# MLA heads of a streaming encoder in another order: probability tiles grouped, weight split behind the gating, sample output transposed last

## The chip, the cores and the metric

The kernel runs on one core of a Trainium2 chip. The metric is the device time of one execution, in microseconds (us). The median of three runs before the change is 2366.46 us (2363.36 to 2369.05).

## What is computed

One step of a two-layer encoder on two inputs: a prompt of 512 new frames and a sample of 64 frames that continues a cache of 512. Layer 1 is forgetting attention with 16 heads, layer 2 is multi-head latent attention (MLA) with 16 heads; both end with an output projection. The change lies in the MLA heads. Cut to what one head computes there:

```python
kv = einsum('bsc,chd->bshd', c, w_ukv)           # latent (512 wide) to keys and values, 128 + 128 a head
kn, v = _rms_norm(kv[..., :128], g_knope), kv[..., 128:]
logits = (qn @ kn.T + qr @ kr.T) * MLA_SCALE      # 128 content columns, 64 rotary ones
p = softmax(where(chunk-causal mask, logits, NEG_INF))
o = (p @ v) * silu(gate)                          # then x + o @ w_out, after all heads
```

The prompt has 512 queries and keys; the sample has 64 queries over 512 + 64 keys.

## The kernel before, in words

`program` runs blocks one after the other: layer 1, its output projection, the latent and the gates (`block_d`), the queries (`block_e`), the MLA heads (`block_f`, about 1709 to 2145 us of the span) and the output projection (`block_g`). All products are made in fp32r with each operand split into a high and a low half: the high half is copied by ScalarE (ACT), the low half is a subtraction on VectorE (DVE), and three products of halves are added up on TensorE (PE).

`block_f` pipelines the heads: one pass works on the attention of head g = h - 1 and, between its steps, on the up-projection of head h, so that PE has matmuls while ACT and DVE turn one step's result into the next one's operand. `MlaHead.ORDER` lists the steps of a pass, and every engine walks the same list, in its own instruction queue. Pass 0 has no attention, pass 16 has no up-projection, and the 15 passes between have both.

Names that begin with T are tiles of the up-projection. T0 to T7 are 12 matmuls of 256 columns each, four key/value tiles from the prompt and four from the cache, two tiles in a bank (banks 0 to 3); T8 is the sample's own 64 rows, in bank 4. ACT squares the keys of a finished bank (`act_keys`), DVE sums the squares (`dve_sums`), GpSimd (POOL) raises them to the power -0.5 (line 2313), DVE scales the keys (`dve_keys`), and ACT and DVE take the values out as halves (`act_values`, `dve_values`). A T tile may write its bank once the values of the head before are out of it, and T0 also waits for the head's weights: `make_hi` on ACT and `make_lo` on DVE split them (line 195, 128x1024), in one buffer that is free after T7.

The other names are jobs of the attention. `qn`, `kp`, `qr` transpose the prompt's queries, keys and rotary queries; `s3` to `s0` are logits of the four query tiles, `sa` and `sb` the sample's logits in two halves; `p3` to `p0` transpose the probabilities by key tile (1, 2, 3 and 4 transposes), `pn` the sample's; `g` transposes the gate; `o` is the prompt's output (12 matmuls of 512 to 256 columns), `on` the sample's (5 of 256), and `ont` transposes the sample's output after DVE has added its parts and gated it. DVE gates `o` while it takes it out of the bank (`o_mla`, line 2198). Behind its part of `p3` DVE also scales the gate by the softmax sums (`dve_scale_gate`).

Jobs share three PSUM banks (5, 6 and 7) by turns: a job's bank is its index in `JOBS` modulo 3, so each job waits until the job three places before it is out of the bank (`wait_operands`), across the passes too. Who lets a bank go: for jobs that are split, DVE after the low half; for `s` jobs ACT after the exponential; for `g` and `ont` ACT; for `o` and `on` DVE.

```python
        own, k = self.job(name)
        count = {own: k - 1}
```

Of the kernel before, what the change touches and what calls it, by code (L numbers as in the profile page):

```python
# [87 lines left out]
def steps(eng, n, body):  # L88

    body(0, n == 1)  # L90
    if n > 2:
        with eng.Fori(1, n - 1) as i:
            body(i, False)
    if n > 1:
        body(n - 1, True)
# [1800 lines left out]
class MlaHead:  # L1896
# [4 lines left out]


    ORDER = ["qn", "kp", "qr", "T0", "T1", "s3", "ka", "T2", "s2", "new", "T3", "s1", "s0", "T8", "sa", "sb", "T4",
             "p3", "T5", "pn", "p2", "p1", "T6", "on", "p0", "g", "T7", "ont", "o"]
    JOBS = [n for n in ORDER if n[0] != "T"]
    SPLITS = ["qn", "kp", "qr", "ka", "new", "p3", "pn", "p2", "p1", "p0"]
    HALF = [slice(0, NT), slice(NT, 2 * NT + 1)]
# [351 lines left out]
def block_f(c, K, S, tail):  # L2259

    nc, d = c.nc, c.dram
    o_all = c.at("o_mla", [HD, HEADS, SEQ + NEW], F32, c.X)
    wplace, xplace = c.packer(S.f_base), c.packer(c.X + 36864)
    H = MlaHead(c, K, S, wplace, xplace)
    assert wplace.cur[0] <= K.base and xplace.cur[0] <= c.Y, (wplace.cur[0], K.base, xplace.cur[0], c.Y)
    G = H.G
    started = lambda g: not isinstance(g, int) or g > 0

    with nc.Block() as block:
        @block.sync  # L2270
        def _(sp):
            def load_q(g):
                if started(g):
                    H.wait_ready(sp, g - 1, "new")
                sp.dma_start(H.q[:], d["queries"][g]).then_inc(H.q_in.sem, 16)

            def load_gate(g):
                if started(g):
                    H.wait_ready(sp, g - 1, "ont")
                cols = bass.ds(g * HD, HD) if not isinstance(g, int) else slice(g * HD, (g + 1) * HD)  # L2280
                for q, t in ((P, slice(0, NT)), (NEW, slice(SM, TT))):
                    sp.dma_start(H.gate[0:q, t, :], d["gates"][0:q, t, cols]).then_inc(H.g_in.sem, 16)

            G.load(sp, 0, 0)
            G.load(sp, 1, 0)


            tail.sp(sp, HEADS // 2 - 2)
            load_q(0)
            tail.sp(sp, HEADS // 2 - 1)  # L2290
            load_gate(0)
            with sp.Fori(1, HEADS - 1) as h:
                G.load(sp, h + 1, 0)
                load_q(h)
                load_gate(h)
            load_q(HEADS - 1)
            load_gate(HEADS - 1)

        @block.gpsimd
        def _(pool):  # L2300
            pool.memset(H.ss[:], 1.0).then_inc(H.zero.sem, 1)
            pool.memset(H.rs[:], 1.0).then_inc(H.zero.sem, 1)
            pool.memset(H.half[:], -0.5).then_inc(H.zero.sem, 1)
            for x in (H.ptn[:], H.v[:, 2 * NT, :, :], H.pt[NT - 1][0][:], H.pt[NT - 1][1][:]):
                pool.memset(x.bitcast(F32), 0.0).then_inc(H.zero.sem, 1)
            pool.wait_ge(H.zero.sem, 7)
            tail.pool(pool)

            def body(h, last):

                for half, t in enumerate(H.HALF):
                    H.var.wait(pool, h, half + 1)
                    pool.tensor_tensor(H.rstd[:, t], H.ss[:, t], H.half[:, t], ALU.pow).then_inc(H.rst.sem, 1)
            steps(pool, HEADS, body)

        @block.scalar
        def _(act_):
            def body(h, last, g):
                for name in H.ORDER:
                    if name[0] != "T":  # L2320
                        if g is not None:
                            H.act_job(act_, g, name, o_all)
                    elif h is not None:
                        if name in ("T1", "T3", "T5", "T7"):
                            H.act_keys(act_, h, int(name[1]) // 2)
                        elif name == "T8":
                            H.act_new_lo(act_, h)
                        elif name == "T4":
                            H.act_new_keys(act_, h)
                    if h is not None:  # L2330
                        if name == "T7" and not last:
                            G.make_hi(act_, h + 1, 0)


                        if name == "o":
                            H.keys.wait(act_, h, 1)
                            if g is not None:
                                H.wait_ready(act_, g, name)
                            for b in (0, 1):
                                H.act_values(act_, h, b)  # L2340

                    if g is not None and name == "qr":
                        H.keys.wait(act_, g, 2)
                        for b in (2, 3, 4):
                            H.act_values(act_, g, b)
            G.make_hi(act_, 0, 0)
            tail.act(act_)
            body(0, False, None)
            act_.wait_ge(H.zero.sem, 7)
            with act_.Fori(1, HEADS - 1) as h:  # L2350
                body(h, False, h - 1)
            body(HEADS - 1, True, HEADS - 2)
            body(None, True, HEADS - 1)

        @block.vector
        def _(dve):
            for bank_free in H.free:
                bank_free.grant(dve)

            def body(h, last, g):  # L2360
                for name in H.ORDER:
                    if name[0] != "T":
                        if g is not None:
                            H.dve_job(dve, g, name, o_all)
                            if name == "p3":
                                H.dve_scale_gate(dve, g)
                    elif name == "T8" and h is not None:
                        H.dve_new(dve, h)
                    if h is not None:
                        if name == "s0":  # L2370
                            H.dve_sums(dve, h, 0)
                        if name == "sb":
                            H.dve_keys(dve, h, 0)
                        if name == "T7":
                            H.dve_sums(dve, h, 1)
                            if not last:
                                G.make_lo(dve, h + 1, 0)
                        if name == "o":
                            for b in (0, 1):
                                H.dve_values(dve, h, b)  # L2380
                    if g is not None and name == "qr":
                        H.dve_keys(dve, g, 1)
                        for b in (2, 3, 4):
                            H.dve_values(dve, g, b)
            G.make_lo(dve, 0, 0)
            tail.dve(dve)
            dve.wait_ge(H.zero.sem, 7)
            body(0, False, None)
            with dve.Fori(1, HEADS - 1) as h:
                body(h, False, h - 1)  # L2390
            body(HEADS - 1, True, HEADS - 2)
            body(None, True, HEADS - 1)

        @block.tensor
        def _(pe):
            def body(h, last, g):
                for name in H.ORDER:
                    if name[0] != "T":
                        if g is not None:
                            H.pe_job(pe, g, name)  # L2400
                    elif h is not None:
                        H.pe_tile(pe, h, int(name[1]))
            body(0, False, None)
            pe.wait_ge(H.zero.sem, 7)
            with pe.Fori(1, HEADS - 1) as h:
                body(h, False, h - 1)
            body(HEADS - 1, True, HEADS - 2)
            body(None, True, HEADS - 1)
    return o_all
# [122 lines left out]
```

## Time and profile before

| | |
|---|---|
| median of 3 runs | 2366.46 us |
| profiled execution: its time | 2365.76 us |
| profiled execution: its span, first to last instruction | 2364.0 us |
| mean granted clock of TensorE | 0.981 |
| PE busy | 2235.4 us (95%) |
| DVE busy | 1142.2 us (48%) |
| ACT busy | 921.4 us (39%) |
| POOL busy | 216.4 us (9%) |

The page gives one execution. The ends of matmuls are modelled, and successive ones overlap in the rows, so that distances are taken from start to start. Idle time of an engine is listed before the instruction that ended it, with the instruction that released it. Times in the rows are microseconds from the start of the span.

### The profile page before, as it was taken

How to read it: one execution, taken by the hardware profiler on the slowest of the kernel's cores; microseconds unless marked ns; L12 is line 12 of the kernel's file. 1: busy time of each engine (PE TensorE's matmuls, PEld its weight loads, DVE VectorE, ACT ScalarE, POOL GpSimd, SP SyncE). 2: the span in 40 equal slices, each digit the busy share in tenths (PEclk: the TensorE clock that was granted, in tenths of full speed). 3: DMA queues.
4: the chain of work that ended last, by engine and by line, in shares of the span. 5: the costliest groups of instructions: out<-in, count | busy, mean ns of one | idle time of the engine just before them, and what ended most of it. 6: DMA issues, size and time to landing. Idle time of an engine off the chain costs nothing. (4 is left out here: it accounts for less than half of the span.)

```text
span 2364.0 us, 33512 instructions
## 1 busy us (share of the span) xinstructions
PE 2235.4 (95%) x11777; PEld 1896.9 (80%) x11777; DVE 1142.2 (48%) x2633; ACT 921.4 (39%) x1968; POOL 216.4 (9%) x234
## 2 busy tenths in 40 slices
PE   7799999999999999998997999997699999997998
PEld 5688888888888888877887878887689899986887
DVE  5444444444445544552223433224567777774222
ACT  5344444444444444442223333224345555543111
POOL 0100000000000000100000000004721111110000
PEclk9899999999999999999998999998999999998999
DMA  4233333333333323324323222323321111113331
GB/s 159 86 97 100 96 97 98 103 103 103 98 103 101 97 95 100 115 73 143 120 83 122 82 88 100 101 82 117 119 96 44 58 46 51 49 37 129 120 129 68
DMA packets 106110, 225.21 MB, mean 95 GB/s; under 512 B 10384, under 2 KB 45456, under 8 KB 105920
## 3 DMA queue, kind: packets, MB, share of 16 engines
q1 hardware_dynamic: 106048, 224.35, 29.2%
q8 instruction: 42, 0.69, 0.1%
q14 instruction: 20, 0.16, 0.0%
HBM read 191.42 MB, written 32.89 MB: 95 GB/s over the span
## 5 line engine op out<-in xcount | busy, mean ns | idle before, releaser
L216 PE MATMUL bank<-b_whi,x_hi 128*128 128x512 f32 x1024 | 413.5, 404 | 9.6 <-DVE b_wlo L199 9.6
L216 PE MATMUL bank<-b_whi,x_lo 128*128 128x512 f32 x1024 | 402.5, 393 | 0.0
L216 PE MATMUL bank<-b_wlo,x_hi 128*128 128x512 f32 x1024 | 402.4, 393 | 0.0
L199 DVE SCALAR_TENSOR_TENSOR b_wlo<-b_raw,g_fox,b_whi 128x512 fp32r<-128x512 f32 x256 | 180.8, 747 | 131.2 <-ACT b_whi L186 129.1
L216 PEld LDWEIGHTS bank<-b_whi,x_hi 128*128 128x128 f32 x1024 | 193.6, 189 | 47.0 <-DVE b_wlo L199 9.6
L216 PEld LDWEIGHTS bank<-b_whi,x_lo 128*128 128x128 f32 x1024 | 193.2, 189 | 42.2
L216 PEld LDWEIGHTS bank<-b_wlo,x_hi 128*128 128x128 f32 x1024 | 193.7, 189 | 33.8
L186 ACT ACTIVATE b_whi<-b_raw,g_fox 128x512 fp32r<-128x512 f32 x256 | 170.4, 714 | 78.6 <-PE bank L216 59.5
L216 PE MATMUL bank<-m_whi,x_hi 128*128 128x512 f32 x320 | 124.9, 390 | 0.8 <-DVE m_wlo L199 0.8
L216 PE MATMUL bank<-m_wlo,x_hi 128*128 128x512 f32 x320 | 124.6, 389 | 0.0
L216 PE MATMUL bank<-m_whi,x_lo 128*128 128x512 f32 x320 | 124.5, 389 | 0.0
L199 DVE SCALAR_TENSOR_TENSOR m_wlo<-m_raw,g_mla,m_whi 128x512 fp32r<-128x512 f32 x80 | 56.6, 748 | 132.9 <-ACT m_whi L186 132.9
L216 PE MATMUL bank<-c_whi,x_hi 128*128 128x512 f32 x256 | 102.3, 400 | 8.9 <-DVE c_wlo L195 8.9
L186 ACT ACTIVATE m_whi<-m_raw,g_mla 128x512 fp32r<-128x512 f32 x80 | 53.4, 715 | 146.0 <-PE bank L216 146.0
L216 PE MATMUL bank<-g_whi,g_ohi 128*128 128x512 f32 x256 | 100.5, 392 | 7.2 <-DVE g_wlo L195 7.2
L195 DVE TENSOR_TENSOR g_wlo<-g_raw,g_whi 128x1024 fp32r<-128x1024 f32 x32 | 39.2, 1224 | 131.9 <-ACT g_whi L182 131.9
L216 PE MATMUL bank<-b_whi,x_smp 128*128 128x512 f32 x256 | 102.6, 401 | 0.0
L216 PE MATMUL bank<-c_wlo,x_hi 128*128 128x512 f32 x256 | 101.6, 397 | 0.0
L216 PE MATMUL bank<-c_whi,x_lo 128*128 128x512 f32 x256 | 101.4, 396 | 0.0
L216 PE MATMUL bank<-g_wlo,g_ohi 128*128 128x512 f32 x256 | 100.2, 392 | 0.0
L216 PE MATMUL bank<-g_whi,g_olo 128*128 128x512 f32 x256 | 100.1, 391 | 0.0
L216 PE MATMUL bank<-b_wlo,x_smp 128*128 128x512 f32 x256 | 100.0, 391 | 0.0
(465 smaller groups left out, 5024.0 us busy)
## 6 DMA issues: line engine op xcount, KB each, us to landing
b_raw<-w_fox SPq DMA_DIRECT2D x128, 512.0 KB, 3.5
m_raw<-w_mla SPq DMA_DIRECT2D x40, 512.0 KB, 3.5
c_raw<-w_out SPq DMA_DIRECT2D x32, 512.0 KB, 3.5
g_raw<-w_out SPq DMA_DIRECT2D x32, 512.0 KB, 3.5
f_raw<-w_ukv SPq DMA_DIRECT2D x16, 512.0 KB, 3.5
queries<-e_q SPq DMA_DIRECT2D x16, 480.0 KB, 3.4
f_q<-queries SPq DMA_DIRECT2D x16, 480.0 KB, 3.3
e_raw<-w_uq SPq DMA_DIRECT2D x16, 384.0 KB, 3.3
```

The lines of the kernel that those rows point to most:

```text
L186: op = eng.activation(hi[:, k, :], raw[:, k, :], ACT.Copy, scale=self.gain[:, K:K + 1])
L195: op = eng.tensor_tensor(lo[:], raw[:], hi32, ALU.subtract)
L199: op = eng.scalar_tensor_tensor(lo[:, k, :], raw[:, k, :], self.gain[:, K:K + 1], hi32[:, k, :], ALU.mult, ALU.subtract)
L216: op = eng.matmul(out, a, w[:, k, :], start=(first and k == 0 and i == 0), stop=(last and k == self.kk - 1 and i == len(pairs) - 1))
```

## The change

The list of steps of a pass is changed, and with it four places in the queues of ACT and DVE. `p3` moves behind T5; `pn` is followed by T6 and the three jobs `p2`, `p1`, `p0`; then come T7, `g`, `on`, `o` and, last, `ont`. The high half of the next head's weights moves on ACT from behind T7 to behind `on`; the low half on DVE from behind T7's sums to behind the gating product of `o`. The values of banks 0 and 1 are taken out in the place of `ont`, the last of the list again.

```diff
     ORDER = ["qn", "kp", "qr", "T0", "T1", "s3", "ka", "T2", "s2", "new", "T3", "s1", "s0", "T8", "sa", "sb", "T4",
-             "p3", "T5", "pn", "p2", "p1", "T6", "on", "p0", "g", "T7", "ont", "o"]
+             "T5", "p3", "pn", "T6", "p2", "p1", "p0", "T7", "g", "on", "o", "ont"]
@@ scalar
-                        if name == "T7" and not last:
+                        if name == "on" and not last:
                             G.make_hi(act_, h + 1, 0)
-                        if name == "o":
+                        if name == "ont":
                             H.keys.wait(act_, h, 1)
                             if g is not None:
-                                H.wait_ready(act_, g, name)
+                                H.wait_ready(act_, g, "o")
                             for b in (0, 1):
                                 H.act_values(act_, h, b)
@@ vector
                         if name == "T7":
                             H.dve_sums(dve, h, 1)
-                            if not last:
-                                G.make_lo(dve, h + 1, 0)
-                        if name == "o":
+                        if name == "o" and not last:
+                            G.make_lo(dve, h + 1, 0)
+                        if name == "ont":
                             for b in (0, 1):
                                 H.dve_values(dve, h, b)
```

The index of each job from the twelfth on, and so its bank, before and after:

| index | 11 | 12 | 13 | 14 | 15 | 16 | 17 | 18 | 19 | 0 | 1 |
|---|---|---|---|---|---|---|---|---|---|---|---|
| bank | 7 | 5 | 6 | 7 | 5 | 6 | 7 | 5 | 6 | 5 | 6 |
| before | p3 | pn | p2 | p1 | on | p0 | g | ont | o | qn | kp |
| after | p3 | pn | p2 | p1 | p0 | g | on | o | ont | qn | kp |

## Rows read from the trace of the kernel before

**Rows 1.** Windows: stretch, length, busy us and instructions by engine, clock, DMA share, GB/s.

```profile
1863.00:1889.00 26.00, 25.37 (x196) 23.55 (x194) 19.53 (x58) 13.40 (x41) 3.20 (x2) 1.00 0.17 51
```

**Rows 2.** Waits from 1709 to 2150 us: total, times, longest.

```profile
DVE f_knlo L2179 <- ACT f_knhi L2118: 21.3, 16, 1.3
...
PE bank L2064 <- DVE o_mla L2198: 9.3, 15, 0.9
```

**Rows 3.** Timeline of PE, end of one pass: start us, duration us, instruction, count, idle.

```profile
1884.24 0.28 PE L2037 MATMUL bank<-f_whi,pc_lo 128*128 128x256 f32 x1
...
1885.15 0.39 PE L2093 MATMUL bank<-f_pt0lo,f_v 128*128 128x512 f32 x1
...
1886.74 0.28 PE L2093 MATMUL bank<-f_pt3hi,f_v 128*128 128x256 f32 x1
...
1888.08 0.65 PE L2064 MATMUL bank<-ident,f_k 128*128 128x128 f32 x4 [0.63 <-DVE o_mla L2198]
1888.66 0.43 PE L84 MATMUL bank<-ident,f_q 128*64 128x128 f32 x2
...
1889.30 0.36 PE L2037 MATMUL bank<-f_whi,c_hi 128*128 128x256 f32 x1
```

**Rows 4.** Timeline of PE in the same pass, from T5 to the gate.

```profile
1878.61 0.28 PE L2037 MATMUL bank<-f_whi,pc_lo 128*128 128x256 f32 x1
1878.82 0.43 PE L84 MATMUL bank<-ident,f_pn 64*128 64x64 f32 x2
1879.09 0.40 PE L85 MATMUL bank<-ident,f_pn 64*128 64x64 f32 x4
1879.42 0.77 PE L2087 MATMUL bank<-ident,f_p 128*128 128x128 f32 x5
...
1881.46 0.76 PE L2097 MATMUL bank<-f_v,f_ptn 128*128 128x256 f32 x5
1882.06 0.60 PE L2087 MATMUL bank<-ident,f_p 128*128 128x128 f32 x4
1882.50 0.60 PE L2102 MATMUL bank<-ident,f_gate 128*128 128x128 f32 x4
```

**Rows 5.** Timeline of ACT in the same pass.

```profile
1877.78 0.26 ACT L2118 ACTIVATE f_pt3hi<-bank 128x128 fp32r<-128x128 f32 x1
1878.93 0.38 ACT L2151 ACTIVATE f_sq<-bank 128x256 f32<-128x256 f32 x1 [0.89 <-PE bank L2037]
...
1884.56 0.38 ACT L2151 ACTIVATE f_sq<-bank 128x256 f32<-128x256 f32 x1 [0.78 <-PE bank L2037]
1884.84 1.05 ACT L182 ACTIVATE f_whi<-f_raw 128x1024 fp32r<-128x1024 f32 x1
```

**Rows 6.** Timeline of DVE in the same pass.

```profile
1878.07 0.29 DVE L2179 TENSOR_TENSOR f_pt3lo<-bank,f_pt3hi 128x128 fp32r<-128x128 f32 x1 [0.46 <-ACT f_pt3hi L2118]
...
1880.05 0.55 DVE L2179 TENSOR_TENSOR f_ptn<-bank,f_ptn 128x256 fp32r<-128x256 f32 x2
...
1883.13 0.28 DVE L2205 TENSOR_TENSOR f_on<-f_on_sum 64x128 f32<-64x128 f32 x1
...
1886.08 1.22 DVE L195 TENSOR_TENSOR f_wlo<-f_raw,f_whi 128x1024 fp32r<-128x1024 f32 x1
1887.26 0.69 DVE L2198 TENSOR_TENSOR o_mla<-bank,f_gt 128x512 f32 x1
1887.86 0.75 DVE L2256 TENSOR_TENSOR f_v<-bank,f_v 128x256 fp32r<-128x256 f32 x2
```

**Rows 7.** Timeline: POOL's power beside DVE's weight split, first attention pass and a later one.

```profile
1756.44 1.17 POOL L2313 TENSOR_TENSOR f_rstd<-f_ss,f_half 128x5 f32<-128x5 f32 x1 [9.63 <-DVE f_ss L2239]
1756.66 1.23 DVE L195 TENSOR_TENSOR f_wlo<-f_raw,f_whi 128x1024 fp32r<-128x1024 f32 x1 [0.30 <-issue]
...
1886.13 2.19 POOL L2313 TENSOR_TENSOR f_rstd<-f_ss,f_half 128x5 f32<-128x5 f32 x1 [10.09 <-DVE f_ss L2239]
```

**Rows 8.** Timeline of PE in the last pass, which has no T tiles.

```profile
2138.68 1.44 PE L2097 MATMUL bank<-f_v,f_ptn 128*128 128x256 f32 x5 [1.10 <-DVE f_ptn L2179]
```

## The prediction

> **What bounds the kernel now.** I read the page first: PE is busy for 95% of the span, DVE and ACT for less than half. The change touches only the MLA heads, so the windows come next: in a pass of 26 us PE is busy 25.37 us at the full granted clock, 2.4 GHz, DVE 19.53 and ACT 13.40 [rows 1]. PE is the bound of a pass, and a pass can only get shorter by less work on PE or by a shorter stop of it. The list of waits has one stop of PE that comes back in each of the 15 mixed passes: the transposes of the keys (`kp`) wait for the gating product on DVE, 9.3 us in all [rows 2]. The timeline shows why: `kp` has the bank of `o`. The last matmul of `o` starts at 1886.74, and the product only at 1887.26, because the low half of the next weights is still in front of it on DVE (1886.08, 1.22 us); `kp` starts at 1888.08 [rows 3, 6]. Work is there for 0.12 us (that matmul) and 0.44 us (`qn`, four transposes), so PE stands for 1888.08 - 1887.30 = 0.78 us. The units: five 256-column matmuls take 1882.06 - 1881.46 = 0.60, so 0.12 each; four transposes take 0.44, so 0.11 each [rows 4].
>
> **Part 1: work on PE.** No matmul is added or dropped; only changes of kind differ. From T7's last matmul to the second of `o` there are 0.91 us; less 0.12 for that matmul and 0.23 for the first 512-column one (an estimate: 512/256 of 0.12, less a little), `ont` costs 0.56 us between matmuls [rows 3]. As the last job of a pass, ahead of transposes, it costs what the first matmuls of `pn` show: 0.09 us to enter (1878.61 + 0.12 to 1878.82) and 0.27 us (to 1879.09), so 0.36 [rows 4]. `pn` now comes behind a transpose and not behind T5. The nearest row is `qr` behind `kp`: 0.58 us less 0.44, so 0.14 to enter against 0.09: +0.05 [rows 3]. That 0.05 lies between 0 and 0.14, and the saving on `ont` between 0 and 0.3.
>
> **Part 2: a new wait, `p0` for `pn`.** By the table of banks `p0` takes bank 5 from `pn`, so it waits until DVE has split `pn`. Before, `on` stood there, which needs that split anyway and had T6 to cover it. On the clock of the pass shown, with T4 where it was: T5 starts 0.11 earlier, its last matmul at 78.50 (1800 left out). ACT's square follows 0.32 after it (1878.61 to 1878.93), ACT's next instruction 0.28 after that (as 1884.56 to 1884.84): `p3`'s high half at 79.10. DVE follows 0.29 later (77.78 to 78.07): 79.39 [rows 4 to 6]. Then comes the scaling of the gate, and `pn`'s split starts 1.98 after `p3`'s; a little of that was waiting for ACT, I take 1.90, so 81.29, done 0.55 later, and seen by PE 0.10 later (an estimate, about what is left of 0.82 after the product's 0.69): 81.94 [rows 6]. PE: T5 done 78.62, `p3` 78.73, `pn` 0.14 + 0.60 to 79.47, then T6, `p2`, `p1`, the same work as from 1879.42 to 1881.46: 2.04, so 81.51 [rows 4]. `p0` waits 0.43 us. It is between 0.2 (scaling no longer than the last head's, earlier sight) and 0.6 (the full 1.98, later sight). Behind it in PE's queue stand T7, `g`, `on` and `o`: all of it is on the path. The other grouped jobs find their banks free: `p1` needs `p3`'s split (79.7), `g` needs `p2`'s, which follows `pn`'s.
>
> **Part 3: the end of a pass.** Now `o` has bank 5, the bank of `qn`, not `kp`'s. The stop moves 0.44 us up, in front of `qn`, and only `ont` (0.36) stands before it. Against that the product no longer waits for the weight split: it starts 0.32 us after the last matmul of `o` starts, as ACT's square does behind a T tile [rows 4, 5], where it took 0.52. From product to the waiting transposes the trace has 0.82 (1887.26 to 1888.08), from the start of `kp` to T0 1.22 [rows 3, 6]. Before: last matmul of `o` to T0 = 1889.30 - 1886.74 = 2.56. After: 0.32 + 0.82 + 0.44 + 1.22 = 2.80, so +0.24; `ont` is hidden in it. If the product were as late as before it would be +0.44; if PE saw it 0.1 us earlier (an estimate), +0.14.
>
> **Part 4: what is moved on DVE and ACT.** The weight split, 1.18 us from its start to the next instruction, now stands behind the product and in front of the values of bank 0, for which T0 waits. Product at 0, split at 0.60, values at 1.78, the first done at 2.20, seen at 2.30 [rows 6]. T0 comes 2.48 after the product: 0.18 us to spare, and the weights themselves are ready over half a microsecond earlier. So I cost it at nothing; each 0.1 us beyond the 0.18 costs 1.5 us over the kernel. The query splits come some 0.9 us later on DVE than before; behind them DVE stands 1.3 us a head for ACT [rows 2], where it catches up. The high half on ACT has a free stretch behind `on`. The loads on SP's queue (weights behind the low half, gate behind `ont`) start up to 2 us later and have most of a pass of 26 us to land.
>
> **Sum.** Per mixed pass: -0.56 (`ont` in front of `o`) + 0.05 + 0.43 + 0.24 = +0.16 us; 15 passes: +2.4 us. In the last pass, a chain without T tiles, `on` (1.44 us there [rows 8]) goes off the way from `pn` to `o` and `ont` off the way to the product; the chain then meets PE's own work and a granted clock that is still low, so I take -0.5, between -1.4 and +0.4. Net +1.9 us on the profiled execution: 2365.8 + 1.9 = 2367.7. The median of the runs lies 0.7 higher; I name 2368.2.
>
> **A rule on the port.** In most passes POOL's power starts at 1886.13, just after the weight split, and lasts 2.19 us; where it began first (1756.44) it lasts 1.17 [rows 6, 7]. The Trainium skill ("SBUF — State Buffer", who interferes with whom) says that a DVE instruction with two SBUF inputs and a GpSimd one that reads SBUF exclude each other, and that the first holds the pair for its whole length. The trace agrees for DVE first (1887.30 + 1.02 is the end of the long one). For POOL first it does not: the split ran from 1756.66 inside POOL's span.
>
> **The rivals.**
> 1. `p0` does not wait: DVE reaches `pn` in time, because PE comes later than I count or the scaling is shorter. For it: only 0.43 us separates them, worked out over eight steps. Against: the scaling is a block of almost 2 us that T5 in front of `p3` pushes 1.2 us later. Then 15 x 0.43 = 6.5 us go: 2361.7.
> 2. Slower: POOL's power holds off DVE. In the new order it starts 1.57 us after the square of T7's bank, some 1.4 us before the product, beside the two short additions of the sample's output (0.28 us each [rows 6]), which read SBUF twice. Held until POOL is done, 0.24 us before the product could start, they still need 0.7 us, and the product comes 0.48 later, on the path: 15 x 0.48 = 7.2 us: 2375. It decides if the hold is longer than 0.8 us; rows 7 speak against it (0.22 us was enough there).
> 3. Slower: DVE's queue from the product to T0's values takes over 2.48 us, by the 0.30 us that the split once stood for issue [rows 7], or the late query splits reach the first logits. At 0.2 us a pass, 3 us: 2371.
> 4. PE's savings are larger and the stops shorter by 0.2 together: 15 x 0.2 = 3 us less than forecast: 2365, no difference to see.
>
> **How the numbers follow.** Forecast 0.45, rival 1 0.16, rival 2 0.08, rival 3 0.16, rival 4 0.15. A measurement of this kernel tells 0.2% from no change, 4.7 us: 2361.7 to 2371.2. Rival 1 lies on that edge, and half of it and a share of rival 4 are faster: 0.14. Rival 2, half of rival 3 and a tail of the forecast are slower: 0.22. The rest is the same: 0.64. The range 2361.5 to 2373 takes in the bounds of parts 1 to 3 (15 x -0.3 to 15 x +0.3) and rivals 1, 3 and 4.
>
> **What would show it.** In the list of waits: PE's transposes of probabilities (L2087) waiting for DVE's `ptn` split, 15 times about 0.4 us; `qn` (L85) waiting for `o_mla`, 15 times about 0.6; no wait of `kp`; passes 0.16 us further apart than before. POOL's power 1.17 us long in every pass. Rival 1 is right if L2087 has no wait; rival 2 if the sample's additions start behind POOL's end; rival 3 if T0 waits for `f_v`. The forecast is wrong if passes come 0.15 us or more closer together than before, or over 0.45 us further apart.

## The result, and the profile after

The changed kernel takes 2371.36 us (median of 20 runs, 2368.27 to 2374.26), the kernel before 2366.61 us (20 runs beside them on the same chip): ratio 1.0020, 95% interval 1.0013 to 1.0027, or 4.75 us slower. The forecast was 2368.2 in a range of 2361.5 to 2373.0, with 0.64 on "same". The time stands in the range and 0.16 us above 2371.2, the upper edge of what the text called the same. The profiled execution took 2371.31 us, its span is 2369.5 against 2364.0.

The same stretch of one pass as in [rows 1], in the windows of the changed kernel (columns as there): still the full clock, and PE stands for 0.85 us of these 26 us (26 less 25.15), where it stood for 0.63.

```profile
1863.00:1889.00 26.00, 25.15 (x195) 23.33 (x194) 19.12 (x58) 13.28 (x40) 2.17 (x2) 1.00 0.17 50
```

Its waits over the MLA heads, against [rows 2]. `kp`'s wait for the product (L2064 for `o_mla`) is gone; `qn` (L85) has it instead, and the transposes of `p0` (L2087) wait for the split of `pn`; the longest of these waits, 1.1 us, is that of the last pass.

```profile
PE bank L85 <- DVE o_mla L2198: 9.0, 15, 0.6
...
PE bank L2087 <- DVE f_ptn L2179: 4.3, 15, 1.1
```

PE in one pass, from T5's end to the last transpose before T0 (start, duration; against [rows 3, 4]):

```profile
1879.52 0.27 PE L2087 MATMUL bank<-ident,f_p 128*128 128x128 f32 x1
1879.72 0.43 PE L84 MATMUL bank<-ident,f_pn 64*128 64x64 f32 x2
...
1881.85 0.71 PE L2087 MATMUL bank<-ident,f_p 128*128 128x128 f32 x5
1882.80 0.66 PE L2087 MATMUL bank<-ident,f_p 128*128 128x128 f32 x4 [0.23 <-DVE f_ptn L2179]
...
1887.57 0.28 PE L2093 MATMUL bank<-f_pt3hi,f_v 128*128 128x256 f32 x1
1887.78 0.43 PE L84 MATMUL bank<-ident,f_on 64*128 64x64 f32 x2
1888.83 0.66 PE L85 MATMUL bank<-ident,f_q 128*128 128x128 f32 x4 [0.62 <-DVE o_mla L2198]
1889.32 0.60 PE L2064 MATMUL bank<-ident,f_k 128*128 128x128 f32 x4
...
1890.49 0.36 PE L2037 MATMUL bank<-f_whi,c_hi 128*128 128x256 f32 x1
```

DVE in the same pass, against [rows 6]:

```profile
1880.30 0.29 DVE L2179 TENSOR_TENSOR f_pt3lo<-bank,f_pt3hi 128x128 fp32r<-128x128 f32 x1 [1.74 <-ACT f_pt3hi L2118]
...
1882.20 0.54 DVE L2179 TENSOR_TENSOR f_ptn<-bank,f_ptn 128x256 fp32r<-128x256 f32 x2
...
1886.85 0.28 DVE L2205 TENSOR_TENSOR f_on<-f_on_sum 64x128 f32<-64x128 f32 x1
1887.24 0.28 DVE L2207 TENSOR_TENSOR f_on<-f_on,f_gate 64x128 f32<-64x128 f32 x1
1888.00 0.69 DVE L2198 TENSOR_TENSOR o_mla<-bank,f_gt 128x512 f32 x1 [0.48 <-PE bank L2093]
1888.61 1.22 DVE L195 TENSOR_TENSOR f_wlo<-f_raw,f_whi 128x1024 fp32r<-128x1024 f32 x1
1889.74 0.75 DVE L2256 TENSOR_TENSOR f_v<-bank,f_v 128x256 fp32r<-128x256 f32 x2
```

The distance of two passes is that of two products: 1888.00 less 1861.82 is 26.18 us, against 25.89 before: +0.29 a pass, where +0.16 was forecast. Split at the last matmul of `o`, the mixed part of a pass (T4 to that matmul) is 10.92 us against 10.99, so -0.07 (forecast -0.08), and the end (that matmul to T0) is 1890.49 - 1887.57 = 2.92 against 2.56, so +0.36 (forecast +0.24).

The last pass, which has no T tiles. The last product starts at 2148.93 (before: 2144.63); from `kp` of this pass to it 24.37 us against 23.86, so +0.5, where -0.5 was forecast. The windows (columns as in [rows 1]) give the clock from the last logits to the product: the changed kernel at 0.63 almost to its end,

```profile
2134.80:2148.40 13.60, 10.80 (x50) 9.43 (x50) 7.27 (x27) 4.90 (x17) 0.00 (x0) 0.63 0.00 0
```

the kernel before at 0.68, and in `o` at the full clock:

```profile
2131.20:2142.00 10.80, 7.92 (x41) 6.31 (x39) 6.71 (x27) 4.47 (x16) 0.00 (x0) 0.68 0.00 0
2142.00:2145.60 3.60, 2.45 (x14) 1.98 (x13) 1.02 (x2) 0.55 (x2) 0.00 (x0) 1.00 0.00 0
```

The same matmul of `o` in PE's timeline, first of the changed kernel, then of the one before, shows it: 0.63 us against 0.39 (the two levels, 1.2 and 2.4 GHz).

```profile
2145.75 0.63 PE L2093 MATMUL bank<-f_pt0lo,f_v 128*128 128x512 f32 x1
...
2148.62 0.28 PE L2093 MATMUL bank<-f_pt3hi,f_v 128*128 128x256 f32 x1
```

```profile
2142.72 0.39 PE L2093 MATMUL bank<-f_pt0lo,f_v 128*128 128x512 f32 x1
```

The sum of the two profiled executions, cut at the starts of `kp`: up to the first `kp` -0.3 us (1730.94 against 1731.25), the 15 mixed passes +4.1 (393.62 against 389.52; 0.29 in most of them, 0.11 in the first), the last pass up to its product +0.5, all behind it +1.2 (block g's first matmuls ran longer at the low clock; more below). That is the 5.5 us.

### The profile page after: what moved, and what is told of

Same layout as the page of the kernel before. It is cut to its first block and busy times, and to the rows that moved or that the text cites. A ratio compares the mean times of both kernels' runs of the same rounds, so it can differ in the third digit from the quotient of the medians.

```text
span 2369.5 us, 33556 instructions
## 1 busy us (share of the span) xinstructions
PE 2240.2 (95%) x11777; PEld 1899.2 (80%) x11777; DVE 1140.7 (48%) x2633; ACT 923.8 (39%) x1968; POOL 203.0 (9%) x234
```

## The experiments

All medians stand beside runs of the kernel before on the same chip (2367.25 us for the first four, 2366.71 for the next four, 2366.40 for e9 to e11). Passes are distances of two products between 1835 and 1970 us. After minus before is +0.29.

**1. Only `p0`'s wait away.** DVE scales the gate behind `pn`'s split and no longer in front of it.

```diff
-                            if name == "p3":
+                            if name == "pn":
                                 H.dve_scale_gate(dve, g)
```

> The changed kernel with one thing moved: the scaling of the gate on VectorE stands behind pn's split and not in front of it, so that bank 5 is free before p0 needs it. Theory (the changed kernel lost 0.40 us a pass to p0's wait for pn's split): the wait of L2087 for f_ptn is gone from the 15 mixed passes, 15 x 0.40 = 6.0 us less than the changed kernel: about 2365.4, just under the kernel before. Rival (VectorE's queue gives it back: the splits of p2, p1 and p0 now stand behind the scaling, and o or g waits for them): half or less of it, 2368.5 or more, with a new wait of L2093 or L2102.

Measured: 2366.39 us, ratio to before 0.9994 (0.9985 to 1.0003). The list has no wait of L2087 but one of 0.5 us in the last pass, passes are 25.73 us apart; two products in DVE's timeline:

```profile
1886.92 0.69 DVE L2198 TENSOR_TENSOR o_mla<-bank,f_gt 128x512 f32 x1 [0.48 <-PE bank L2093]
1912.65 0.69 DVE L2198 TENSOR_TENSOR o_mla<-bank,f_gt 128x512 f32 x1 [0.48 <-PE bank L2093]
```

So this one wait costs 26.18 - 25.73 = 0.45 us a pass, and 6.6 us over the 15 mixed passes of the two profiled executions (393.62 against 387.04). By the medians, each against its own kernel before, it is 4.75 + 0.86 = 5.6 us. Without the wait no difference from the kernel before can be told.

**2. The weight split back to its old place.** The changed kernel, with both halves behind T7 again (shown is DVE's; ACT's goes back likewise).

```diff
-                        if name == "o" and not last:
-                            G.make_lo(dve, h + 1, 0)
+                            if not last:
+                                G.make_lo(dve, h + 1, 0)      # under: if name == "T7"
```

> The changed kernel with both halves of the next head's weight split put back behind T7 (ScalarE behind T7's squares, VectorE behind T7's sums). Theory (behind the gating is the right place once on and o come after T7): the 1.2 us split now stands in front of the sample's additions and of the gating product, the product starts about 0.8 us later and qn with it: 14 x 0.8 = 11 us more than the changed kernel, about 2382. Rival (the new place of the split is part of the loss, through T0's wait for weights and values): faster than the changed kernel by 1 to 4 us, 2367 to 2370.

Measured: 2383.22 us, 1.0069 (1.0055 to 1.0082), passes 26.89. The larger wait is now that of `ont` (L84), not the product's:

```profile
PE bank L84 <- DVE f_on L2207: 13.1, 14, 1.3
...
PE bank L85 <- DVE o_mla L2198: 5.2, 15, 0.4
```

The place of the split is worth 0.7 us a pass to the new order. This part of the change earns its keep; it pays for itself only in that order, as the next shows.

**3. The split alone.** The kernel before, with the low half behind the product.

```diff
                         if name == "T7":
                             H.dve_sums(dve, h, 1)
-                            if not last:
-                                G.make_lo(dve, h + 1, 0)
                         if name == "o":
+                            if not last:
+                                G.make_lo(dve, h + 1, 0)
```

> The kernel before with only VectorE's half of the weight split moved behind the gating product; the order of the steps is the old one. Theory: the product starts 0.09 us earlier, kp too, but the values of bank 0 come 1.7 us after the product and T0 has to wait for them, to about 0.13 us later than before: 14 x 0.13 = +1.9 us, about 2368.5, with T0 (L2037) waiting for f_v in most passes. Rival (the split in front of the product is what kp waits for, so taking it away is a gain by itself): 1.3 us or more less than before, 2365.3 or less, and no wait of T0.

Measured: 2373.79 us, 1.0025 (1.0014 to 1.0037), passes 26.18. Right in sign, larger in size. PE's last matmul of `o` starts at 1891.58, and DVE, idle before it, starts the product 0.61 us later, not 0.32:

```profile
1892.19 0.69 DVE L2198 TENSOR_TENSOR o_mla<-bank,f_gt 128x512 f32 x1 [1.30 <-PE bank L2093]
```

That was the first sign of the failed size. The product is 0.10 us later behind `o` than before (0.62 against 0.52), and T0 then does wait, as expected, for the values: it starts at 1894.41, 0.06 us after the first half of `f_v` (1893.93 + 0.42), 2.21 us behind the product where it was 2.04.

**4 and 5. `ont` last alone, then with the split.** The kernel before with `o` and `ont` exchanged; e5 moves DVE's split behind the product too.

```diff
-              "p3", "T5", "pn", "p2", "p1", "T6", "on", "p0", "g", "T7", "ont", "o"]
+              "p3", "T5", "pn", "p2", "p1", "T6", "on", "p0", "g", "T7", "o", "ont"]
```

> The kernel before with only the last two jobs exchanged (o, then ont, with the values taken out behind ont); probability tiles and weight split stay where they were. Theory: o ends 0.56 us earlier, but the product still stands behind the weight split (start unchanged), and qn, which now has the bank of o, waits for it: T0 0.45 us later a pass, 15 x 0.45 = +6.8 us, about 2373. Rival (transposing the sample's output last saves its 0.56 us on TensorE whatever follows): 3 us or more less than before.

Measured: 2374.25 us, 1.0028 (1.0019 to 1.0038), passes 26.29, and `qn` waits as expected:

```profile
PE bank L85 <- DVE o_mla L2198: 14.6, 15, 1.3
```

> The kernel before with the last two jobs exchanged (o, then ont) and VectorE's half of the weight split behind the gating product; p tiles in the old places, ScalarE's half behind T7 as before. Theory: o ends 0.56 us earlier, nothing stands in front of the product, which starts 0.43 us after o's last matmul starts, T0 2.92 after it (both as in the changed kernel): 1889.10 where the kernel before has 1889.30, so 0.20 a pass, passes 25.7 us apart, about 2.9 us less than before: 2364.4. Rival (the split behind the product costs by itself, as the run with only the split moved seems to say): T0 waits for f_v again, no gain, 2367 or more.

Measured: 2370.91 us, 1.0017 (1.0008 to 1.0026), passes 26.10. A miss by 6.5 us, 0.4 us a pass. `T0` waits for nothing, but the product, on an idle DVE, again starts 0.62 us behind `o`'s last matmul (1888.95), and `qn` waits 0.8 us a pass for it. That is 0.19 of the 0.4.

```profile
1889.57 0.69 DVE L2198 TENSOR_TENSOR o_mla<-bank,f_gt 128x512 f32 x1 [0.96 <-PE bank L2093]
```

The rest is on PE. With `o` right behind T7, its second matmul starts 0.56 us after T7's last, where 0.35 (0.12 + 0.23) was counted on, so the mixed part of a pass falls by 0.34 us and not by 0.56 (10.64 against 10.98), here and in e4:

```profile
1886.80 0.28 PE L2037 MATMUL bank<-f_whi,pc_lo 128*128 128x256 f32 x1
...
1887.36 0.40 PE L2093 MATMUL bank<-f_pt0lo,f_v 128*128 128x512 f32 x1
```

**6. The grouping alone.** The kernel before in the order T5 p3 pn T6 p2 p1 p0 on g T7 ont o.

```diff
-              "p3", "T5", "pn", "p2", "p1", "T6", "on", "p0", "g", "T7", "ont", "o"]
+              "T5", "p3", "pn", "T6", "p2", "p1", "p0", "on", "g", "T7", "ont", "o"]
```

> The kernel before with only the grouping: T5, p3, pn, T6, p2, p1, p0, on, g, T7, ont, o; weight split and end of the pass as before. Theory (grouping makes p0 wait for pn's split in bank 5): L2087 waits for f_ptn 0.4 us in each of the 15 mixed passes, +0.45 us a pass, passes 26.3 us apart, about 6.5 us more than before: 2373.5. Rival (fewer changes between transposes and matmuls save as much as the wait costs): within 2 us of before.

Measured: 2377.43 us, 1.0045 (1.0032 to 1.0059), passes 26.46, that is +0.57. Both waits stand in the list:

```profile
PE bank L2064 <- DVE o_mla L2198: 9.3, 15, 0.8
...
PE bank L2087 <- DVE f_ptn L2179: 3.9, 15, 0.7
```

Grouping brings `p0`'s wait (0.40 us, as in the changed kernel) without any other edit. The other 0.17 is PE's: in this order `on` and `g` stand between `p0` and T7, so there are more changes between transposes and matmuls than before, and the rival's case of fewer changes was not tested. Alone the three edits cost 0.57 (grouping), 0.40 (`ont` last, e4) and 0.29 (split, e3) a pass, together 0.29: they don't add. From e5 (26.10) to the changed kernel, which groups and also moves `g` and `on` behind T7, it is +0.08, and to e1, without `p0`'s wait, -0.37. Of this 0.37, 0.17 is PE's mixed part (10.64 to 10.47) and 0.19 the product, which starts 0.43 and no longer 0.62 us behind `o`.

**7 and 8. The order of waits inside an instruction's code.** e7 is the changed kernel with, in the source, the wait that ends last put last: for `qn` and `kp` the one on the bank, for the product the one on `o`; e8 is e7 with the edit of e1.

```diff
+        elif name == "qn":
+            self.q_in.wait(eng, g, 1)
         self.wait_operands(eng, g, name)
...
-            self.wait_ready(eng, g, name)
             self.wait_out_of(eng, g, "g")
+            self.wait_ready(eng, g, name)
```

> The changed kernel with the waits of two steps in another order, nothing else: the gating product waits first for the gate's bank, which is free early, and then for o; qn waits first for its loaded queries and then for its bank; kp for the keys first. Theory (in the loop the waits' values are computed in registers, and what is computed behind a wait that has just passed is on the path: the product starts 0.43 us after o's last matmul in the loop and 0.31 outside it): product and qn together 0.1 to 0.2 us earlier a pass, 1.5 to 2.8 us less than the changed kernel, about 2369.3, passes 26.0 us apart. Rival (the 0.12 us is the engine's own start after a wait, whatever stands behind it): no difference from the changed kernel, 26.17.

Measured: 2371.75 us, 1.0022 (1.0012 to 1.0031), passes 26.17. A miss: `qn` comes 0.75 us behind the product and not 0.83, but the product 0.50 behind `o`'s last matmul (1892.24) and not 0.43.

```profile
1892.74 0.69 DVE L2200 TENSOR_TENSOR o_mla<-bank,f_gt 128x512 f32 x1 [0.55 <-PE bank L2095]
```

DVE's queue shows why: the waits don't stand in it as in the source. In the changed kernel a semaphore step passes at 1887.5, before `o`'s last matmul starts (1887.57), so it waits for the gate's bank, and the wait for `o` is that of the address step at 1887.9, the last one. In e7 the semaphore step itself starts only 0.32 us behind `o`'s last matmul, and the address step comes behind it. So e7 put the wait that ends last first on DVE, and last on PE. First the changed kernel, then e7:

```profile
L74 DVEq EVENT_SEMAPHORE  x1: 21/21/21, 1887.5 to 1887.5; - x1
L2198 DVEq FUSED_REGOPS  x1: 64/64/64, 1887.9 to 1887.9; - x1
```

```profile
L74 DVEq EVENT_SEMAPHORE  x1: 21/21/21, 1892.6 to 1892.6; - x1
L2200 DVEq FUSED_REGOPS  x1: 64/64/64, 1892.6 to 1892.6; - x1
```

> The changed kernel with the gate's scaling behind pn's split and the waits in the order of the run before. Theory: both gains add, passes 25.73 - 0.15 = 25.58 us apart, 2.1 us less than with the scaling moved alone: about 2364.3, faster than the kernel before by 0.12%. Rival: the order of the waits does nothing, 2366.4.

Measured: 2365.01 us, 0.9996 (0.9987 to 1.0005), passes 25.73, as e1 and not 25.58: the 0.08 us that `qn` gains and the 0.07 that the product loses cancel again.

**9 to 11. What is left to win at the end of a pass.** e9 is e1 with one bank number skipped before `g`, so that `qn` no longer shares `o`'s bank (the first cut below). e10 is e1 with e7's order for PE alone. e11 is both, with the low half of the split made in two pieces (the second).

```diff
     def job(self, name):
+        i = self.place_of(name)
+        return i % 3, sum(1 for n in self.JOBS if self.place_of(n) <= i and self.place_of(n) % 3 == i % 3)
+
+    def place_of(self, name):
         i = self.JOBS.index(name)
-        return i % 3, i // 3 + 1
+        return i + (i >= self.JOBS.index("g"))
```

```diff
+                        if name == "on" and not last:
+                            G.half_lo(dve, h + 1, 0)
                         if name == "o" and not last:
-                            G.make_lo(dve, h + 1, 0)
+                            G.half_lo(dve, h + 1, 1)
```

> The changed kernel with the gating multiplication behind pn (as in e1_gate_later, 25.73 us a pass) and one bank number skipped ahead of g: g moves to bank 7, on to 5, o to 6, ont to 7, and the next pass's qn stands in a bank that the product does not hold; kp stands behind o instead. My theory (what is left at the end of a pass is the wait of the first tile behind ont for the product): qn starts right behind ont, 0.2 to 0.5 us earlier; kp then waits for the product, and T0 for f_v, which ends some 2.3 us after the product. Passes of 25.5 us, in all about 2363.3 us. Rival (the product, not PE, sets the pace at the end of a pass, whichever tile waits for it, because f_v behind it gives T0 its data): passes stay at 25.7, in all 2366.

Measured: 2365.37 us, 0.9993 (0.9984 to 1.0002), passes 25.67: nearer to the rival. `qn` starts right behind `ont`, but the start of `kp` to T0 takes 1888.34 - 1886.95 = 1.39 us, against 1.17 in the changed kernel: T0 starts 0.06 us after the first half of `f_v` is done (1887.86 + 0.42). T0 is 0.19 us nearer to `o` than in e1, though the product starts 0.52 us behind `o` and not 0.43, and the rest of the pass is 0.13 longer, 0.09 of it between the gate's transposes and `on`. The trace points to the bank: `on` now has bank 5 behind `p0`, whose split on DVE ends at 1882.96, and starts 0.14 us later, at 1883.10. That was not tested.

```profile
1886.95 0.65 PE L2068 MATMUL bank<-ident,f_k 128*128 128x128 f32 x4
...
1888.34 0.39 PE L2041 MATMUL bank<-f_whi,c_hi 128*128 128x256 f32 x1
```

```profile
1882.29 0.67 DVE L2183 TENSOR_TENSOR f_pt0lo<-bank,f_pt0hi 128x512 fp32r<-128x512 f32 x1
...
1886.12 0.69 DVE L2202 TENSOR_TENSOR o_mla<-bank,f_gt 128x512 f32 x1 [0.59 <-PE bank L2097]
1886.73 1.22 DVE L195 TENSOR_TENSOR f_wlo<-f_raw,f_whi 128x1024 fp32r<-128x1024 f32 x1
1887.86 0.75 DVE L2260 TENSOR_TENSOR f_v<-bank,f_v 128x256 fp32r<-128x256 f32 x2
```

> e1_gate_later with the waits of qn and kp in another order for PE alone (the data first, the bank last); the product's waits on DVE stay as in the changed kernel. In e7_wait_order qn came 0.08 us sooner behind the product and the product 0.07 later behind o. My theory (the two effects are separate, one on PE, one on DVE): the first without the second, passes of 25.65 us, 2365.2 us. Rival (they are one effect, the place of the product in the queue): passes as in e1_gate_later, 25.73 us, 2366.4 us.

Measured: 2364.55 us, 0.9990 (0.9981 to 0.9999), passes 25.67. `qn` is 0.75 behind the product and the product still 0.43 behind `o`: two separate effects, one per engine, and with DVE's queue left alone the gain of 0.06 to 0.08 us a pass stays.

> e9_banks with the waits of e10_pe_wait and the low half of the weight split computed in two pieces, one behind on's eviction and one behind the product, so that less of DVE's work stands between the product and f_v. My theory: with the bank free, T0 waits for f_v alone, and this takes about 0.25 us from it: passes of 25.25 us, 2360 us, which would be under both kernels. Rival (T0 does not wait for f_v, or the added instruction costs what it saves): as e9_banks, 25.5 us and 2363.3 us, or above.

Measured: 2360.35 us, 0.9972 (0.9961 to 0.9982), passes 25.41, expected 25.25. It is 6.05 us faster than the kernel before and the fastest here. The first half of the split fills the time in which DVE stood for `o`, and T0 comes 1889.44 - 1886.95 = 2.49 us behind `o`'s last matmul. DVE's timeline:

```profile
1886.79 0.69 DVE L208 TENSOR_TENSOR f_wlo<-f_raw,f_whi 128x512 fp32r<-128x512 f32 x1
1887.47 0.69 DVE L2211 TENSOR_TENSOR o_mla<-bank,f_gt 128x512 f32 x1
1888.07 0.68 DVE L208 TENSOR_TENSOR f_wlo<-f_raw,f_whi 128x512 fp32r<-128x512 f32 x1
1888.67 0.75 DVE L2269 TENSOR_TENSOR f_v<-bank,f_v 128x256 fp32r<-128x256 f32 x2
```

**12. The failed size by itself.** The changed kernel with the product written to a fixed place inside the loop, so that its address is a constant. Its output leaves out the heads of the loop.

```diff
-            self.release(eng.tensor_tensor(dst[:, g, 0:SEQ], b[:, :], self.gt[:], ALU.mult), name)
+            k = g if isinstance(g, int) else 0
+            self.release(eng.tensor_tensor(dst[:, k, 0:SEQ], b[:, :], self.gt[:], ALU.mult), name)
```

> The changed kernel, but in the loop over the heads the product is written to the place of head 0, whatever the head (a memset of the heads so left out stands once behind the loop, so the last passes and block g do not count), so that DVE computes no address for it. My theory: the 0.43 us between the start of o's last matmul and the product is 0.31 us (as in the unrolled last pass but one, 2123.01 to 2123.32) and 0.12 us of address computation that stands behind the wait; without it the product starts 0.31 to 0.34 us behind o's last matmul and the passes are 26.06 to 26.09 us apart instead of 26.18. Rival (the 0.12 us is the wait itself, whose value is in a register in the loop, or another cost of the loop): 0.43 us and 26.18 us stay.

Measured: passes 26.06 to 26.07 us, the product 0.32 us behind `o`'s last matmul. The one time, 2378.8 us, has the memset (5.61 us, on DVE) in it. PE's end of a pass, then DVE's products:

```profile
1890.23 0.28 PE L2093 MATMUL bank<-f_pt3hi,f_v 128*128 128x256 f32 x1
1890.44 0.43 PE L84 MATMUL bank<-ident,f_on 64*128 64x64 f32 x2
1891.38 0.65 PE L85 MATMUL bank<-ident,f_q 128*128 128x128 f32 x4 [0.50 <-DVE o_mla L2199]
```

```profile
1890.55 0.69 DVE L2199 TENSOR_TENSOR o_mla<-bank,f_gt 128x512 f32<-128x512 f32 x1 [0.36 <-PE bank L2093]
1916.62 0.69 DVE L2199 TENSOR_TENSOR o_mla<-bank,f_gt 128x512 f32<-128x512 f32 x1 [0.37 <-PE bank L2093]
```

The waits, with their values in registers and in the order of the changed kernel, cost nothing more; the address does. The changed kernel's DVE queue shows the step, 64 ns each, once per pass of the loop (14 passes; the fifteenth and the last are unrolled):

```profile
L2198 DVEq FUSED_REGOPS  x14: 64/64/64, 1757.0 to 2097.3; - x14
```

The same reading fits the other kernels. Wherever DVE stands empty there, the first step of its queue that has to wait for `o` starts 0.32 us behind the start of its last matmul; what stands behind that step decides. Nothing: the product at 0.32 (e12). Only the address step is that step: 0.43 (changed kernel, e1, e10). A semaphore step, then the address: 0.50 (e7, e8). A register step of the waits (ALU_OP), then the address: 0.52 in e9, and 0.62 in e3 and e5, where the address step starts 0.19 us behind it and not 0.09; why, the trace doesn't say. Only the address step was tested by itself, in e12.

The last pass of this run is of use too. Its order is that of the changed kernel, but here `o` ran at the full clock but for its first matmul: the same matmul as above takes 0.40 us, from `o`'s first matmul to the product it is 2.27 us (2154.86 to 2157.13), and from `kp` to the product 23.05.

```profile
2155.22 0.40 PE L2093 MATMUL bank<-f_pt0lo,f_v 128*128 128x512 f32 x1
```

## Why the prediction was right or wrong

- **Part 1, PE's work: right in sum.** The mixed part came out at -0.07 for a forecast of -0.08 (-0.56 + 0.05 + 0.43), and without `p0`'s wait (e1) at -0.51 for -0.56 + 0.05. How it divides is less sure: `ont` put last in the old order saved 0.34 and not 0.56 (e4, e5), so in the changed kernel some 0.2 of the -0.51 comes with the other moves, for which the forecast had a small cost.
- **Part 2, `p0` waits for `pn`'s split: right**, in its size too. DVE split `pn` 1.90 us behind `p3`, as taken, and PE followed 0.06 us after its end, where 0.10 was taken. Five transposes from 1881.85 end at 1882.40, the next start at 1882.80: 0.40 us for a forecast of 0.43. e1 takes the wait away and gets 0.45 back, and e6 has it without the other edits. Rival 1 is out.
- **Part 3, the end of a pass: right in its mechanism, and one size failed.** The forecast was 0.32 + 0.82 + 0.44 + 1.22 = 2.80 us. It measured 0.43 + 0.83 + 0.49 + 1.17 = 2.92. The step that failed is "it starts 0.32 us after the last matmul of `o` starts, as ACT's square does behind a T tile". The square writes to a fixed place; the product's address is computed from the loop's register. In the kernel before that ran while DVE had the weight split in hand (address step at 1887.1, the split's end at 1887.30). Now DVE stands empty, and the computation comes after the wait. Moving a wait to an idle engine uncovered what its queue does behind the wait. The unrolled pass (0.31) and e12 (0.32) show it. It is 14 x 0.11 = 1.5 us, one for each pass of the loop. The 0.50 to 0.62 of e3, e5, e7 and e9 have more steps behind that wait; this is read from the traces, not tested.
- **Part 4, costed at nothing: right.** T0 started 0.33 us after the first half of `f_v` was done (1889.74 + 0.42 to 1890.49). Rival 3 is out in the changed kernel; in e3, and in e9 with the bank out of the way, the values are what T0 waits for.
- **The last pass: wrong in sign in this execution.** The order did free `on` and `ont`, but "a granted clock that is still low" was taken for 0.5 us of loss only. The clock stayed at the low level through `o` into its last but one matmul: from `o`'s first matmul to the product it took 3.60 us (2145.33 to 2148.93), before 2.25 (2142.38 to 2144.63). Without these 1.35 us the last pass would be 0.85 shorter than before. e12 bears this out: in the same order, with `o` at the full clock, it is 0.81 shorter (23.05 against 23.86). So the order saves what the forecast hoped for, and whether `o` still meets the low clock decides the sign; in the changed kernel, e2 and e7, all of this order, most of `o` ran at the low clock (3.60, 3.20 and 3.68 us to the product). What keeps the clock low was not tried. Block g's start was also longer at the low clock in this execution (0.50 and 0.72 in two stretches of 4 us, where before had 0.59 and 1.00). One execution each was profiled, and stretches with the same code differ between the profiled executions of this document: the heads' first T0 starts between 1713.75 (e8) and 1719.44 (e7), and all behind the last product takes 218.96 (e8) to 220.61 us. So I don't claim these 1.2 us for the change.
- **Rival 2, POOL holds DVE: not seen.** POOL's power now starts first in each of the 15 mixed passes, as it had to for this rival, and the two short DVE instructions of the sample's output inside its span (an addition and the gating, both with two SBUF inputs) have the length and distance of before (0.28 us each, 0.39 apart).

```profile
1886.50 1.17 POOL L2313 TENSOR_TENSOR f_rstd<-f_ss,f_half 128x5 f32<-128x5 f32 x1 [9.36 <-DVE f_ss L2239]
```

The Trainium skill ("SBUF — State Buffer", who interferes with whom) has the first of the pair take the shared port for its whole length and the other wait. The trace doesn't agree for POOL first: the two instructions at 1886.85 and 1887.24 ran inside 1886.50 to 1887.67; with DVE first the trace had agreed [rows 7].

- **The sum.** The chance of "slower" was 0.22. The 15 mixed passes came out 1.7 us above the forecast (4.1 against 2.4), the last pass 1.0; with both the forecast is 2368.2 + 1.7 + 1.0 = 2370.9, against 2371.36. The last 0.4 is not a proof: the 1.2 us of block g and the earlier start of the heads are in the profiled execution too.

## What to carry to other kernels

When a job is moved so that its wait now ends on an idle engine, what that engine's queue still has to do after the wait (here an address from a loop register) gets a price of its own: take the delay from a row with the same addressing. When transposes are moved together, see which job their banks come from and what the engine that frees them does in between: here moving DVE's gate scaling by one place was worth 0.45 us a pass, 5.6 us by the medians, more than the whole reordering cost (4.75). Read the order of the waits in front of an instruction from its queue and not from the source, and have the one that ends last stand last. When a wait can't be removed, fill it (e11: half a split in the gap) before trying to shorten it.

## What was not expected of the hardware

- An address from a register behind a passed wait on an idle engine: 0.43 us from the start of the last matmul to DVE's start in the loop, 0.32 with a constant address, 0.31 in an unrolled pass.
- The order of the waits in an engine's queue: with the one that ends last behind the others it is 0.75 us from the product to the transposes on PE, otherwise 0.83; on DVE 0.43 from the matmul to the product, otherwise 0.50 (e7, e10). The order in the queue was not always that of the source.
- One 128x1024 DVE subtraction takes 1.13 us to the next instruction (e9, 1886.73 to 1887.86), one of 128x512 takes 0.60 (e11, 1888.07 to 1888.67): two halves cost 0.07 us more than the whole.
